# The opening of a decoder trunk kernel: h made on ScalarE straight from PSUM, x normed in place and transposed, the first half of the channels tile by tile, half a slab on the matrix engine

## The reference

```python
c_act = jax.nn.silu(c)
mod = c_act @ ada_w[layer] + ada_b[layer]            # 1024 -> 6 * 1024
sh_m, sc_m, ga_m, sh_f, sc_f, ga_f = jnp.split(mod, 6, axis=-1)
h = rms_norm(x, norm_g[layer, 0]) * (1.0 + sc_m) + sh_m
# gdn_mixer:
proj = h @ w_in                                      # 1024 -> 4112, the first tiles of it are queries
qkv = jax.nn.silu(causal_dwconv(qkv, conv_w))
```

## Time and profile before

| | |
|---|---|
| median of 3 runs | 1375.21 us |
| span of the profiled execution, first to last instruction | 1374.7 us |
| PE busy | 1316.5 us, 96% |
| DVE, ACT, POOL busy | 823.7, 569.7, 126.3 us |
| mean granted clock of PE over the span | 0.987 |
| first product with `w_in` | 39.6 us |
| second half of the first quad begins | 57.95 us |

### The profile page before, as it was taken

One profiled execution on the slowest core, in us unless ns is written; L12 is line 12 of the kernel. 1 busy time (PEld: TensorE's weight loads), 2 busy tenths in 40 slices (PEclk: granted clock), 3 DMA queues, 4 the chain that ended last, 5 costly groups with the idle time before them and its releaser, 6 DMA issues. The chain is left out here.

```text
span 1374.7 us, 18203 instructions
## 1 busy us (share of the span) xinstructions
PE 1316.5 (96%) x7011; PEld 1080.8 (79%) x7011; DVE 823.7 (60%) x1436; ACT 569.7 (41%) x1085; POOL 126.3 (9%) x142
## 2 busy tenths in 40 slices
PE   3799999999999999999999999999999999999998
PEld 3668788889798888888888866656888888888886
DVE  4879787557577655665656769776463323333335
ACT  3356674555453212221224665675353213222231
POOL 1002020005300000000000011130000000000000
PEclk9899999999999999999999999999999999999999
DMA  9644522110516555564532211010122223322321
GB/s 323 203 159 149 184 66 89 63 62 4 182 62 231 200 180 184 184 214 154 184 125 90 84 33 33 30 62 1 62 92 92 92 92 118 97 92 70 115 92 62
DMA packets 102856, 158.39 MB, mean 115 GB/s; under 512 B 9325, under 2 KB 74106, under 8 KB 102778
## 3 DMA queue, kind: packets, MB, share of 16 engines
q1 hardware_dynamic: 91898, 115.40, 25.6%
q0 software_dynamic: 10880, 41.95, 8.9%
HBM read 155.24 MB, written 2.10 MB: 114 GB/s over the span
## 5 line engine op out<-in xcount | busy, mean ns | idle before, releaser
L401 PE MATMUL ps<-h_hi,w_hi 128*128 128x512 f32 x872 | 344.6, 395 | 0.4 <-ACT tmp L1054 0.4
L403 PE MATMUL ps<-h_hi,w_lo 128*128 128x512 f32 x872 | 341.4, 391 | 0.0
L402 PE MATMUL ps<-h_lo,w_hi 128*128 128x512 f32 x872 | 341.1, 391 | 0.0
L385 DVE TENSOR_TENSOR w_lo<-raw,w_hi 128x1024 fp32r<-128x1024 f32 x172 | 209.4, 1223 | 210.6 <-ACT w_hi L379 208.9
L379 ACT ACTIVATE w_hi<-raw 128x1024 fp32r<-128x1024 f32 x174 | 182.4, 1051 | 142.6 <-PE ps L2083 137.3
L403 PEld LDWEIGHTS ps<-h_hi,w_lo 128*128 128x128 f32 x872 | 164.7, 189 | 35.0
L401 PEld LDWEIGHTS ps<-h_hi,w_hi 128*128 128x128 f32 x872 | 164.9, 189 | 33.7 <-issue 0.5
L402 PEld LDWEIGHTS ps<-h_lo,w_hi 128*128 128x128 f32 x872 | 165.0, 189 | 33.5
L504 DVE SCALAR_TENSOR_TENSOR ada_acc<-ada_in,c_act,ada_acc 128x512 f32<-128x512 f32 x154 | 115.5, 750 | 4.2
L1944 ACT ACTIVATE g_hi<-tmp 128x512 fp32r<-128x512 f32 x44 | 27.8, 632 | 201.0 <-DVE tmp L1979 201.0
L2081 PE MATMUL ps<-w_hi,g_hi 128*128 128x512 f32 x256 | 100.1, 391 | 0.0
(11 more groups left out here) (387 smaller groups left out, 2145.4 us busy)
## 6 DMA issues: line engine op xcount, KB each, us to landing
raw<-in_ffn_w_in_dram SPq DMA_DIRECT2D x44, 1024.0 KB, 5.2
ada_in<-in_ada_w_dram POOLq DMA_DIRECT2D x40, 1024.0 KB, 5.6
raw<-in_ffn_w_out_dram SPq DMA_DIRECT2D x20, 1024.0 KB, 5.0
raw<-in_gdn_w_in_dram SPq DMA_DIRECT2D x16, 1024.0 KB, 5.8
ada_in<-in_ada_w_dram SPq DMA_DIRECT2D x4, 1024.0 KB, 9.5
x_t<-in_x_dram SPq DMA_DIRECT2D x2, 2048.0 KB, 10.0
early_slab<-in_ada_w_dram SPq DMA_DIRECT2D x4, 1024.0 KB, 14.3
raw<-in_gdn_w_out_dram SPq DMA_DIRECT2D x4, 1024.0 KB, 4.9
```

The costliest lines, as they stand in the source:

```text
L385: ops.tensor_tensor(lo, raw_tile(s, kc) if src is None else src, f32(hi), ALU.subtract).then_inc(lo_done, 1)
L401: nc.tensor.matmul(out_, hi[:, k, :], r_hi[:, k, :], start=k == 0, stop=False)
L402: nc.tensor.matmul(out_, hi[:, k, :], r_lo[:, k, :], start=False, stop=False)
L403: last = nc.tensor.matmul(out_, lo[:, k, :], r_hi[:, k, :], start=False, stop=k == kc - 1)
```

## The change

Seven edits to the opening; nothing behind the first quad is changed, except that semaphore counts are shifted.

1. x is normed in place: DVE scales the token blocks 0 and 1, ACT the blocks 2 and 3, each 128x1024. The diagonal matrix is gone, and PE turns x with plain transposes (one record a block in place of two). All four blocks are waited for.
2. The order of the turned tiles is 7, 0, 1, 2, 3, then PE's sum of slab 2, then 4, 5, 6. Every tile but 7 has a PSUM bank of its own and stays there.
3. ACT makes h out of PSUM twice per tile, once rounded into `h_hi` and once whole into `h_raw`, each time with scale and shift from SBUF. DVE's scaling of h and ACT's copies are gone; DVE only subtracts.
4. DVE's first half of slab 2 stands before the root, its second half after the scaling of x.
5. On DVE one weight split stands before the four subtractions of h, three behind them; on ACT the roundings are put between the tiles of h.
6. The first half of the first quad goes tile by tile: s = 0 with channel tiles 0 to 3, then s = 1 and so on, each waiting for its own weight split.
7. Of slab 3, DVE sums only the first half. PE multiplies the second half itself, with 16 one-column float32 matmuls in the middle of the quad (`pe_ada_direct`), and then sums slab 3 and slab 1.

```diff
-        def pe_first_quad(pe, q, r_hi, r_lo, ready, before=None, after=None, between=None, middle=None):
+        def pe_first_quad(pe, q, r_hi, r_lo, ready, after=None, middle=None):
             side = 4
-            pe.wait_ge(lo_done, q * 4 + 4)
...
-            for k in range(side):
-                ready(k)
-                for s in range(4):
+            for s in range(4):
+                pe.wait_ge(lo_done, q * 4 + s + 1)
+                for k in range(side):
+                    if s == 0:
+                        ready(k)
                     product(s, k)
...
+        def pe_ada_direct(pe):
+            pe.wait_ge(slab_here(3)[1], 32)
+            for n in range(4):
+                for k in range(4):
+                    nc.tensor.matmul(ps[:, 7, 4 + n:5 + n], slab_place(3)[1][:, k, n * P:(n + 1) * P],
+                                     c_act[:, 4 + k:5 + k], start=n == 0 and k == 0, stop=False, skip_group_check=True)
...
-            for d in range(DC):
-                act.wait_ge(sem("h_mm"), d + 1)
-                nc.scalar.activation(h_raw[:, d, :], ps[:, d % 4, :], ACT.Copy).then_inc(sem("h_affine"), 1)
-                if d % 2:
-                    act_split(act, 0, d // 2)
-            for d in range(DC):
-                act.wait_ge(sem("h_scaled"), d + 1)
-                nc.scalar.activation(h_hi[:, d, :], h_raw[:, d, :], ACT.Copy).then_inc(sem("h_rounded"), 1)
+            act.wait_ge(sem("row_root"), 1)
+            for b in (2, 3):
+                nc.scalar.activation(x_t[:, b, :], x_t[:, b, :], ACT.Copy, scale=row_rinv[:, 0, b:b + 1])\
+                    .then_inc(sem("x_scaled"), 1)
...
+        def act_first_h(act, d):
...
+            src = h_raw[:, d, :] if d == DC - 1 else ps[:, d, :]
+            for dst, signal in ((h_hi, "h_rounded"), (h_raw, "h_affine")):
+                nc.scalar.activation(dst[:, d, :], src, ACT.Identity, scale=coef[:, 0, 0, d:d + 1],
+                                     bias=shift(0, 0, d)).then_inc(sem(signal), 1)
...
-            nc.vector.tensor_tensor(diag[:, :, :], over_heads(ident[:, :]), along(row_rinv[:, 0, :]),
-                                    ALU.mult).then_inc(sem("x_diag"), 1)
+            for b in range(2):
+                nc.vector.tensor_scalar(x_t[:, b, :], x_t[:, b, :], row_rinv[:, 0, b:b + 1], None, ALU.mult)\
+                    .then_inc(sem("x_scaled"), 1)
...
-            pe.wait_ge(sem("x_diag"), 1)
-            for d in range(DC):
-                if d == 6:
+            pe.wait_ge(sem("x_scaled"), NB)
+            for d in (DC - 1, 0, 1, 2, 3, 4, 5, 6):
+                if d == 4:
                     pe_ada(pe, 2)
...
-                    last = nc.tensor.matmul(ps[:, d % 4, b * P:(b + 1) * P], x_t[:, b, d * P:(d + 1) * P],
-                                            diag[:, b, :], start=True, stop=True)
+                    last = nc.tensor.transpose(ps[:, 4 if d == DC - 1 else d, b * P:(b + 1) * P],
+                                               x_t[:, b, d * P:(d + 1) * P], ident[:, :])
...
         def late_shift(pe):
+            pe_ada_direct(pe)
+            pe_ada(pe, 3)
             pe_ada(pe, 1)
-            pe_ada(pe, 3)
...
+            dve_ada_out(dve, ch, 0)
+            for part in range(2):
+                dve_ada(dve, ch, 2, part)
             dve_first_root(dve)
```

More of the change, by code:

```diff
@@ L463, in product @@
                 return nc.tensor.matmul(ps[:, s, :], lo, r_hi[:, k, :], start=False, stop=k == DC - 1)
-            for k in range(side):
-                ready(k)
-                for s in range(4):
+            for s in range(4):
[3 more added lines that the diff above has]
+                        ready(k)
                     product(s, k)
[L469 to L472, removed]
+            middle()
             for s in range(4):
@@ L505, in dve_ada @@
                                                          ada_sum(j)[:, :], ALU.mult, ALU.add)
-                if k == 3:
+                if k == 3 and isinstance(j, int) and j == 3:
+                    ins.then_inc(ada_used, 2)
+                    dve.wait_ge(ada_used, 8)
+                elif k == 3:
                     ins.then_inc(ada_used, 1)
@@ L726, in diag_no @@
         def diag_no(m, b):
-            return 3 + 6 * m + b - (1 if m >= 2 else 0)
+            return 2 + 6 * m + b - (1 if m >= 2 else 0)
         def turn_no(m, b, g):
@@ L2733, in _ @@
                 dve_ada(dve, ch, 0, part)
+            dve_ada_out(dve, ch, 0)
+            for part in range(2):
+                dve_ada(dve, ch, 2, part)
             dve_first_root(dve)
-            dve_ada_out(dve, ch, 0)
-            for part in range(4):
+            for part in range(2, 4):
                 dve_ada(dve, ch, 2, part)
-            for s in range(4):
+            dve_ada_out(dve, ch, 2)
+            dve_first_coef(dve, 0)
+            dve_split(dve, 0, 0)
+            for d in range(4):
+                dve_first_low(dve, d)
+            for s in range(1, 4):
                 dve_split(dve, 0, s)
-            dve_ada_out(dve, ch, 2)
-            dve_coef(dve, ch, 0, [0], 0, 4)
-            dve_first_h(dve, 0)
             for part in range(4):
                 dve_ada(dve, ch, 1, part)
-            for part in range(4):
+            for part in range(2):
                 dve_ada(dve, ch, 3, part)
@@ L2749, in _ @@
             dve_ada_out(dve, ch, 3)
-            dve_coef(dve, ch, 0, [0], 4, 8)
-            dve.wait_ge(sem("shift_out"), 1)
-            dve_first_h(dve, 4)
+            dve_first_coef(dve, 4)
+            for d in range(4, DC):
+                dve_first_low(dve, d)
+            h_here(dve, 0, DC - 1)
             dve.wait_ge(sem("ba_rounded"), 1)
```

59 lines of the change are left out of this document (35 added, 24 removed).

## The result

The kernel after takes 1381.63 us, the median of 4 executions (1380.67 to 1382.95), against 1375.61 for the kernel before in the same session (4 executions, 1374.97 to 1377.2): a ratio of 1.0043, 95% interval 1.003 to 1.0055, so it is slower by 6.0 us. 1378.6 was forecast, with "slower" as the likeliest. The direction was right; the shift was +3.4 in the forecast and +6.0 in the runs.

A forecast was written before the change was run, and what follows sets the result against it. PE, busy 96% of the span, was taken to bound the kernel. R 2.6 later plus 0.8 behind it made +3.4: span 1374.7 + 3.4 = 1378.1, with 0.5 added 1378.6 us; range 1373.8 to 1382.

The forecast's parts named there:

- root on DVE: DVE's root, behind four operations on slab 2's first half, starts at 25.9 in place of 21.83.
- x scaled by ACT: ACT's scaling of two 128x1024 blocks of x takes 2.2 us, bounds 2.0 and 2.3.
- coefficient: After the turn and PE's sum of slab 2, the coefficient comes at 36.1 against 37.46 before.
- first half ends on PE: PE ends the first quad's first half at 52.8 instead of 53.34.
- DVE ends slab 3's half: DVE sums slab 1 and half of slab 3 by 55.7, 1.4 later than 54.28.
- 32 records on PE: The 16 one-column matmuls in the quad's middle take 3.3 us, at 0.10 a record.
- both sums, to DVE: PE's two sums, 0.95 each, reach DVE at 57.9, 2.4 later than 55.50.
- R: Start of the first quad's second half on PE: 60.5, 2.6 later than 57.95.
- behind R: DVE starts the convolution at R + 7.2 in place of R + 6.44; the 0.8 goes to PE.
- rival of the fast turn: Clock rises within the transposes; R at 58.3 to 59.5, +0.6 to +2, about 1376.3; chance 0.25.
- bound of 6.8 for the records: Upper bound in us for the 32 one-column records in the middle, at the low clock's 0.213 each.
- low-clock rival: Transposes do not lift the clock, s = 1 at 0.43 too; R 62 to 63, about +5.8, 1381; chance 0.17.

The follow-up runs named there:

- e1: The changed kernel with DVE's root put back ahead of both halves of slab 2; 1379.53 us, ratio to before 1.0024.
- e11b: The changed kernel with the 32 transposes of x made as plain float32 matmuls against the identity; 1383.44 us, ratio to before 1.0064.
- e7: The changed kernel with ACT's four weight roundings ahead of the coefficient and two of DVE's splits in its waits; 1378.72 us, ratio to before 1.0019.
- e2: The changed kernel with slab 3 summed wholly on DVE, no one-column matmuls, PE's two sums in the old order; 1381.12 us, ratio to before 1.0036.
- e3: The changed kernel with the 16 one-column matmuls dealt out, four behind each output tile of the first half; 1379.22 us, ratio to before 1.0025.
- e4: The changed kernel without the 16 one-column matmuls, so one scale lacks slab 3's second half; 1379.18 us, ratio to before 1.0027.
- e8: e6 with the 16 matmuls dealt out behind channel tiles 0 to 3 of s = 0, slab 3 loaded and slab 1 summed first; median 1378.14 us, two heaps.
- e5: The changed kernel with the edits of e1 and e3 together; 1376.52 us, ratio to before 1.0007.
- e6: The changed kernel with the edits of e5 and e7 together; 1374.77 us, ratio to before 0.999.
- e9b: e8 with the unrounded h of channel tiles 4 to 7 made on DVE from PSUM in place of ACT; 1378.99 us, ratio to before 1.0013.
- e10b: e6 with the unrounded h of channel tiles 4 to 7 made on DVE in place of ACT; 1374.84 us, ratio to before 0.9995.
- e12b: The same kernel as e8, run again for a second profile; 1381.14 us.

## Why the prediction was right in direction and too small

| step | predicted | measured |
|---|---|---|
| root on DVE | 25.9 | 25.66 |
| x scaled by ACT | 2.2 us | 2.19 |
| turn starts | 29.5 | 29.29 |
| coefficient | 36.1 | 34.72 |
| first product | 38.4 | 37.30 |
| first half ends on PE | 52.8 | 51.62 |
| DVE ends slab 3's half | 55.7 | 54.38 |
| 32 records on PE | 3.3 us | 4.70 |
| both sums, to DVE | 57.9 | 59.98 |
| R | 60.5 | 63.01 |
| behind R | +0.8 | +0.71 |

**Right.** The root waits for slab 2: it starts at 25.66, 3.8 later than before (forecast 4.1), and by that order alone e1 has the turn 4.1 earlier and the end of the first half 3.0. The scaling of x is off by 0.01. The transposes began at the low rate, 0.21 each. Behind R the convolution starts at R + 7.14 (forecast R + 7.2, before R + 6.44), and the sum behind it is 0.7 later for it. PE's wait in front of that sum is 1.02 and not the 1.6 of the forecast, since PE comes there later too: 0.2 is a new wait at 73.86, and the products behind R took 0.2 more. No gap of PE behind 80 us changed by over 1 us; the one for `eu` is 1.97 against 2.00.

**Early where it was forecast late.** The coefficient came 1.4 sooner: the rate rose within the turn, so the last of the 20 transposes and the sum of slab 2 went at half the price (0.82 for eight records in place of 1.7). That is the forecast's rival of the fast turn. The first half went at the high rate from its start (0.47 us for the first product in place of 0.77, and 8.31 us for the 36 from 43.31), where 0.43 a matmul had been assumed up to 44. Together 1.2 at the end of the first half.

**The step that was mis-sized** is the middle, "3.3 us" for the 32 records and "0.95 each" for the two sums: 5.1 us from 52.8 to 57.9. It took 8.36, from 51.62 to 59.98: 1.4 more for the records and 1.85 more for the sums, since both ran on behind the fall of the granted clock at 53.8. How dear it gets differs between executions: the same 48 records took PE 8.25 us in after, 7.2 in e1, 6.5 in e11b and 5.4 in e7. The bound of 6.8 for the records held, but was not carried on to the two sums behind them, which the same clock prices. The kernel before had shown the fall too: its row of the clock reads 0.50 from 55.7 to 62.5, just behind its two sums. In the 14 profiled executions here the clock falls between 2.2 and 5.5 us after the last real product of the first half, whether PE has one-column matmuls then (after 2.2, e7 5.5) or, but for one sum, sits idle (e2 2.2). What matters is how much one-column work still lies behind that product: 32 + 16 = 48 records in after (5.4 us at the high rate, by e7), 16 and a group of 8 in e3 (2.7), 16 in before (2.05). The longer that stretch, the more of it the fall can reach. e3 (dealt out: R 3.76 earlier), e4 (left out: the sums back at 0.9 each) and e7 (the fall late: 5.4 in place of 8.25) show it from three sides. From there to R it was 3.03 in place of 2.6: ACT could start 0.73 after the sum was in, where 0.46 was forecast, its two operations took 1.55 in place of 1.47, and the forecast's own terms add up to 2.7. -1.2 + 3.25 + 0.45 is the 2.5 by which R was missed.

**The low-clock rival** named the right time (1381, R 62 to 63) for reasons of which only the last held. The transposes did lift the clock and s = 1 ran at 0.23 a matmul. Here the Trainium skill's rule in "TensorE: Matmul & The Clock Gate", Part 4, that a PE transpose isn't counted as busy time, disagrees with the trace: the rate doubled 4.0 us into transposes alone, in e1, e3, e7 and e8 after 2.9 to 3.2 us, and with plain matmuls after 4.4 (before) and 5.5 (e11b). These are float32 transposes, and the page's figures there are of bf16. The measurement decides.

**The base.** The shift was added to a median of three executions, 1375.21; the median over more is 1375.6. That is the 0.4 between the 3.0 by which 1378.6 missed and the 2.6 by which the shift did. The offset of 0.5 between span and time was wrong (it is 1.6), but it cancels.

**Where the 6.0 us are.** In the profiled executions the turn starts 5.3 later, but the first half ends 1.7 earlier (51.62 against 53.34). From there it is +6.8 to R (11.4 in place of 4.6) and +0.7 behind R: -1.7 + 6.8 + 0.7 = 5.8. The root's 4.1 is in the -1.7: without it the first half would end 3.0 earlier still (e1). At the end of the span it is 4.6. Further on the granted clock is at 0.50 for 20 us in all, against 24 in before; that this gives the other 1.2 is not shown. The rest is which executions were profiled: before's was 0.7 above its median, after's 0.7 below, and 4.6 + 1.4 = 6.0.

## What to carry to other kernels

A row of tiny matmuls behind the last real product doesn't hold the clock: price it, and everything that stands behind it on the same engine, at both rates. Dealt out between the products it may cost nothing. But settle first whether the engine has come up to its full rate there: before it has, the same dealing out holds it down. A wait moved ahead of a step that feeds the critical chain (here slab 2 ahead of the root) makes that step late by the whole wait, however small the work; what comes of it at the end depends on what would have held the chain next (4.1 us at the turn here, 3.0 at the end of the first half). When the times of one kernel lie in two heaps, take a second profile before a theory: one execution tells only of its own heap.

## What the runs showed of the hardware

- After an idle start PE runs at half its rate, and comes to the full rate 2.9 to 3.2 us into its work (e1, e7, e8, e3), 3.7 (e4), 4.0 to 4.1 (after, e2), 4.4 (before) or 5.5 (e11b). In e5, e6, e9b, e10b and e12b it had not by the end of the first 20 transposes (4.5 us); in e6 it had behind the gap, in the others not. The code is the same in e8 and e12b. The rows print a granted clock of 1.00 for this first stretch, but the trace has no record of the clock there (in after the first is at 33.3, where the rate doubles): the records' pace tells.
- Not having come up by the gap behind the turn, PE came up at 37.7 under plain products (e5, e10b), but only at 50.7 and 51.6 with groups of eight one-column records between them (e12b, e9b). Once up, the same mix ran at the full rate to its end (e8). In e1 and e8 the clock fell again at 31.5 and 31.8, behind a gap of 1.4 and 1.3, and was back at 34.9 and 35.2.
- Behind the last product of the first half the granted clock fell after 2.2 to 2.4 us (after, e2, before), 2.8 to 3.4 (e1, e3, e5, e6, e8), 3.9 to 4.4 (e9b, e10b, e11b, e12b) or 5.4 to 5.5 (e4, e7), with PE busy on one-column matmuls or idle, and came back 3.3 to 5.9 us after the products began again. What decides within these ranges is open.
- One-column float32 matmuls take 0.10 to 0.11 us a record at 2.4 GHz (e3, e7) and 0.20 to 0.21 at 1.2 GHz (e12b, after), two records each.
- A 128x512 read of PSUM on ACT with scale and shift from SBUF takes 0.78 us in after, against 0.60 for a plain copy; two follow 0.67 apart.
